# A hybrid decoder layer on one core: latent attention with its values made in token order, the keys of two heads in a bank of their own, its heads written out, and three weight splits moved

## The reference, cut to what matters

```python
x = x + 0.5 * swiglu(rms_norm(x, g1), ...)                  # up/gate 1024 -> 2816, down 2816 -> 1024
proj = rms_norm(x, g2) @ w_in                               # c_q 384, c_kv 256, k_rope 32, q_d/k_d/v_d, gates 2 x 1024
q  = rms_norm(c_q) @ w_uq      # 8 heads x (64 plain + 32 rotary)
kv = rms_norm(c_kv) @ w_ukv    # 8 heads x (64 for the key + 64 for the value)
y_a = causal_softmax(q, [k_nope, rope(k_rope)]) applied to v, then @ w_br_mla       # "latent attention"
y_b = dilated windowed attention of 3 x 8 heads @ w_br_dil
x = x + (sigmoid(g_a) * y_a + sigmoid(g_b) * y_b) @ w_out
x = x + 0.5 * swiglu(rms_norm(x, g3), ...)
y = rms_norm(x, g4)
```

## Time and profile before

| | us |
|---|---|
| median of 3 runs (1281.72 to 1281.84) | 1281.73 |
| the profiled execution's own time | 1280.79 |
| its span, first to last instruction | 1279.0 |
| PE busy in the span | 1267.3 (99%) |
| DVE, ACT, POOL busy | 669.7, 441.7, 18.8 |
| DMA | 118.38 MB, mean 93 GB/s |
| mean granted TensorE clock | 0.998 |

### The profile page before, as it was taken

The page is one execution under the profiler, slowest core; times in us unless marked ns, Lnnn a source line. Parts: engine busy times, 40 slices in busy tenths (PEclk is TensorE's granted clock), DMA queues, the critical chain, the costliest instruction groups (busy, mean ns, idle before and its releaser), DMA issues.

```text
span 1279.0 us, 16611 instructions
## 1 busy us (share of the span) xinstructions
PE 1267.3 (99%) x5998; PEld 1033.5 (81%) x5998; DVE 669.7 (52%) x984; ACT 441.7 (35%) x763; POOL 18.8 (1%) x36
## 2 busy tenths in 40 slices
PE   9999999999999999999999999999999999999997
PEld 6888888888888777788888888888888888888886
DVE  6744444433336677475665746675644444443323
ACT  6233332322233444343343424423433332232221
POOL 0000000000000000300000000000000000000000
PEclk9999999999999999999999999999999999999999
DMA  6342223333322221622222231222322322233321
GB/s 214 101 111 98 98 98 98 90 91 95 103 92 71 64 70 66 132 67 83 79 78 92 66 99 51 97 89 95 99 96 98 98 98 98 98 90 92 93 88 66
DMA packets 36003, 118.38 MB, mean 93 GB/s; under 512 B 4680, under 2 KB 4680, under 8 KB 35968
## 3 DMA queue, kind: packets, MB, share of 16 engines
q1 hardware_dynamic: 34416, 114.83, 27.8%
q0 software_dynamic: 1264, 3.06, 1.5%
q10 hardware_dynamic: 288, 0.03, 0.0%
HBM read 115.36 MB, written 2.55 MB: 92 GB/s over the span
## 4 chain that ended last, share of the span: by engine, by line
PE 94%; DVE 2%; DMA 1%; issue 1%; ACT 1%; SPq 0%; DVEq 0%; ACTq 0%
PE bank L542 36%; PE bank L376 17%; PE bank L378 17%; PE bank L377 17%; PE bank L725 1%; PE bank L751 1%; PE bank L645 1%; PE bank L672 1%; DVE mla_stats L1451 1%; DMA x<-in_x_t 1%; PE bank L661 1%; PE bank L769 1%; PE bank L765 1%; DMA const<-in_tables 0%; ACT w_hi L358 0%
## 5 line engine op out<-in xcount | busy, mean ns | idle before, releaser
L363 DVE TENSOR_TENSOR w_lo<-raw,w_hi 128x1024 fp32r<-128x1024 f32 (+2 forms) x221 | 258.8, 1171 | 227.6 <-ACT w_hi L358 225.4
L358 ACT ACTIVATE w_hi<-raw 128x1024 fp32r<-128x1024 f32 (+2 forms) x221 | 224.3, 1015 | 433.3 <-PE bank L542 228.3
L542 PE MATMUL bank<-act_hi,w_hi 128*128 128x512 f32 x704 | 218.5, 392 | 0.3 <-DVE w_lo L363 0.3
L542 PE MATMUL bank<-act_hi,w_lo 128*128 128x512 f32 x704 | 217.0, 389 | 0.0
L542 PE MATMUL bank<-act_lo,w_hi 128*128 128x512 f32 x704 | 216.9, 389 | 0.0
L376 PE MATMUL bank<-act_hi,w_hi 128*128 128x512 f32 x528 | 210.7, 399 | 2.0 <-DVE w_lo L363 1.2
L378 PE MATMUL bank<-act_hi,w_lo 128*128 128x512 f32 x528 | 206.2, 390 | 0.0
L377 PE MATMUL bank<-act_lo,w_hi 128*128 128x512 f32 x528 | 205.9, 390 | 0.0
L542 PEld LDWEIGHTS bank<-act_hi,w_hi 128*128 128x128 f32 x704 | 132.2, 188 | 29.6 <-DVE w_lo L363 1.0
L542 PEld LDWEIGHTS bank<-act_hi,w_lo 128*128 128x128 f32 x704 | 132.2, 188 | 27.5
L542 PEld LDWEIGHTS bank<-act_lo,w_hi 128*128 128x128 f32 x704 | 132.2, 188 | 27.4
(11 more groups left out here) (177 smaller groups left out, 1049.3 us busy)
## 6 DMA issues: line engine op xcount, KB each, us to landing
raw<-in_ffn_up SPq DMA_DIRECT2D x87, 512.0 KB, 3.3
raw<-in_w_dil SPq DMA_DIRECT2D x40, 512.0 KB, 3.3
raw<-in_ffn_down SPq DMA_DIRECT2D x32, 448.0 KB, 3.3
raw<-in_ffn_down SPq DMA_DIRECT2D x16, 512.0 KB, 3.5
raw<-in_w_mla_gates SPq DMA_DIRECT2D x8, 512.0 KB, 3.3
raw<-in_w_branches SPq DMA_DIRECT2D x8, 512.0 KB, 3.3
raw<-in_w_out SPq DMA_DIRECT2D x8, 512.0 KB, 3.2
raw<-in_w_latent SPq DMA_DIRECT2D x6, 512.0 KB, 3.3
```

The source lines that it names most:

```text
L358: nc.scalar.activation(w_hi[:, s % SPLIT, 0:tiles * P], raw[:, s % RAW, 0:tiles * P], ACT.Copy).then_inc(hi_ready, 1)
L363: nc.vector.tensor_tensor(w_lo[:, s % SPLIT, 0:tiles * P], raw[:, s % RAW, 0:tiles * P], w_hi[:, s % SPLIT, 0:tiles * P].bitcast(F32), ALU ...
L542: last = nc.tensor.matmul(out, w[:, s % SPLIT, tile * P:(tile + 1) * P], moving[:, row, :], start=row == 0 and w is w_hi and moving is act_hi,
```

## The change

- **Values.** A new piece `w_values` (8 tiles, the value columns of `w_ukv` for all heads) stands ahead of head 0. `values()` makes four chunks of 128 tokens by 512 value features, with the latents as the stationary and the weights as the moving operand: 4 x 2 x 3 = 24 matmuls of 128x512 into banks 5, 6, 2 and 3. ACT scales and copies them to `mla_v` in four activations. `turn_values`, `mla_vt`, L1444 and the copies of L1017 are gone.
- **Keys.** The keys of heads 2p and 2p+1 are one product of 2 tiles (6 matmuls) into bank 7, made with the query of head 2p; DVE takes both in `take_keys(p)`, which stands ahead of the scaling of head 2p-1. Pieces of even heads have 5 tiles, of odd heads 3. The gate chunk no longer shares a bank with keys.
- **Queries.** In even heads DVE takes the next query before the scaling of the probabilities, in odd ones after it.
- **Turning.** PE turns the first seven blocks before the eighth gate tile (k == 7) in even heads, before the seventh in odd ones.
- **Heads.** All eight are written out on every engine, without loops.
- **Splits.** In head 7 ACT rounds the second dilated piece before the exponentials, and DVE takes its remainder before the scaling. After each head ACT rounds the next gate piece before the tanh and no longer after it. In FFN 1, piece 4 is rounded before the first SiLU, and DVE takes its remainder right after its first product with that chunk.

The last hunk below is of DVE's `attention`, the others are PE's.

```diff
+            def values():
+                s = PIECES["mla"]
+                pe.wait_ge(lo_ready, s + 1)
+                pe.wait_ge(chunk_taken, CHUNKS["latent"] + 4)
+                for b, out in enumerate((5, 6, 2, 3)):
+                    block_of = slice(b * P, (b + 1) * P)
+                    for k in range(KKV):
+                        hi, lo = (w[:, s % SPLIT, k * SEQ:(k + 1) * SEQ] for w in (w_hi, w_lo))
+                        latent, rest = (part[:, KQ + k, block_of] for part in (lat_hi, lat_lo))
+                        nc.tensor.matmul(bank[out][:, :], latent, hi, start=k == 0, stop=False)
+                        nc.tensor.matmul(bank[out][:, :], latent, lo, start=False, stop=False)
+                        last = nc.tensor.matmul(bank[out][:, :], rest, hi, start=False, stop=k == KKV - 1)
...
+            def lora(h):
+                s = lora_piece(h)
+                pe.wait_ge(lo_ready, s + 1)
+                if h % 2 == 0:
+                    if h == 0:
+                        pe.wait_ge(mean_ready, 2)
+                    elif h > 2:
+                        pe.wait_ge(mixed_taken, h // 2 - 1)
+                    multiply(s, range(KQ, LORA_TILES), bank[7][:, :], lambda k: lat_hi[:, KQ + k, :],
+                             lambda k: lat_lo[:, KQ + k, :]).then_inc(inner_done, 1)
+                c = query_chunk(h)
+                free_chunk(pe, c)
+                multiply(s, range(KQ), bank[c % 2][:, :], lambda k: lat_hi[:, k, :],
+                         lambda k: lat_lo[:, k, :]).then_inc(piece_done, 1)
...
-            def turn_values(h, i):
...
             def score(h):
-                if h % 2:
-                    pe.wait_ge(turned_taken, 4 * h + 8 * i - 1)
                 pe.wait_ge(head_ready, h + 1)
+                if h == 0:
+                    pe.wait_ge(values_taken, BLOCKS)
...
             def attend(h):
+                if h < MLA_HEADS - 1:
+                    pe.wait_ge(keys_taken, h // 2 + 2)
...
                 def turn_early(k):
-                    if k == 6:
+                    if k == (6 if h % 2 else 7):
...
             def attention(h):
                 maxima(h)
+                if h == MLA_HEADS - 1:
+                    split_lo(dve, PIECES["dil"] + 1, 0, TILES)
+                    normalize(h)
+                    split_lo(dve, PIECES["dil"] + 2, 0, TILES)
...
+                    if h % 2:
+                        take_keys(h // 2 + 1)
+                        normalize(h)
+                        take_query(h + 1)
+                    else:
+                        take_query(h + 1)
+                        normalize(h)
```

More of the change, by code:

```diff
@@ L428, in _ @@
                 load(sp, PIECES["latent"] + q, 0, w_latent[q], TILES)
[L430 to L439, removed]
+            load(sp, PIECES["mla"], 0, w_values, TILES)
+            for h in range(MLA_HEADS):
+                at, tiles = (h % 2) * LORA_TILES * P, lora_tiles(h)
+                load(sp, lora_piece(h), 0, w_lora_up[h // 2, :, at:at + tiles * P], tiles)
+                load(sp, lora_piece(h) + 1, 0, w_mla_gates[h], TILES)
             with sp.Fori(0, PAIRS) as i:
@@ L609, in _ @@
             token_sums(sumsq, bank[7]).then_inc(norm_full, 1)
[L612 to L620, removed]
@@ L622, in turn_values @@
-            def turn_values(h, i):
[L625 to L631, removed]
-                if h % 2:
-                    pe.wait_ge(turned_taken, 4 * h + 8 * i - 1)
-                pe.wait_ge(head_ready, h + 2 * i + 1)
+            def values():
[10 more added lines that the diff above has]
+                        last = nc.tensor.matmul(bank[out][:, :], rest, hi, start=False, stop=k == KKV - 1)
+                    if b < BLOCKS - 1:
+                        last.then_inc(values_done, 1)
+                last.then_inc(piece_done, 1)
@@ L1053, in _ @@
[L1053 to L1057, removed]
+                    split_hi(act, PIECES["dil"] + 1, 0, TILES)
+                exponentials(h)
+                if h < MLA_HEADS - 2:
+                    split_hi(act, lora_piece(h + 2), 0, lora_tiles(h))
+                elif h == MLA_HEADS - 2:
+                    split_hi(act, PIECES["dil"], 0, TILES)
+                else:
+                    split_hi(act, PIECES["dil"] + 2, 0, TILES)
@@ L1255, in up_turn @@
                             dve.wait_ge(own, so_far())
-                    else:
+                    elif not (first and f == 0):
                         split_lo(dve, s + 2, 4 * i, TILES)
@@ L1780 @@
     up_q = given["w_uq"][0].reshape(Q_LORA, MLA_HEADS, QK_DIM)
-    up_kv = _tiles(given["w_ukv"][0])
+    up_kv = given["w_ukv"][0].reshape(KV_LORA, MLA_HEADS, QK_NOPE + V_DIM)
+    put("w_values", up_kv[:, :, QK_NOPE:].reshape(KKV, P, MLA_HEADS * V_DIM).transpose(1, 0, 2).reshape(P, TILES * P))
     rows = []
-    for h in range(MLA_HEADS):
-        query = np.concatenate([up_q[:, h, :QK_NOPE], _swapped(up_q[:, h, QK_NOPE:])], axis=1)
-        rows.append(np.concatenate([_tiles(query)[0], up_kv[h]], axis=1))
+    for pair in range(MLA_HEADS // 2):
+        first, second = (_tiles(np.concatenate([up_q[:, h, :QK_NOPE], _swapped(up_q[:, h, QK_NOPE:])], axis=1))[0]
+                         for h in (2 * pair, 2 * pair + 1))
+        keys = _tiles(up_kv[:, 2 * pair:2 * pair + 2, :QK_NOPE].reshape(KV_LORA, 2 * QK_NOPE))[0]
+        rows.append(np.concatenate([first, keys, second], axis=1))
     put("w_lora_up", np.stack(rows))
```

234 lines of the change are left out of this document (116 added, 118 removed).

## The result

The changed kernel takes 1273.01 us in the median of 4 runs (1272.48 to 1273.69), the kernel before 1281.78 beside it (4 runs, 1281.72 to 1283.47): a ratio of 0.9929, 95% interval 0.9911 to 0.9946. Timed again in a later comparison it took 1272.84 against 1281.23, ratio 0.9933 (0.9916 to 0.9949). The profiled executions took 1280.79 and 1272.62, 8.2 us apart.

The account below looks back on a forecast made before the run. PE, busy 99% of the span, was taken as the bound. Terms 3.0 + 1.4 + 1.3 + 0.3 - 0.2 = 5.8 us took the median from 1281.73 to 1275.9 us; range 1274.3 to 1278.6.

Parts of the forecast that it names:

- transposes: Eight heads each lose four PE transposes of the values, 0.38 us a head: 3.0 us saved, bounds 2.1 and 3.7.
- the gate's bank: PE's gate matmul no longer waits for DVE to empty a shared bank in heads 0, 1, 3, 5: 1.4 us saved.
- head 7: PE's wait between the two dilated pieces goes because the second is split earlier: 1.3 us saved, at least 1.2.
- first turn: PE's idle time before piece 4 goes with its split ahead of the SiLU: 0.3 us saved, bounds 0 and 0.4.
- even heads: DVE's scaling ends only 0.15 us ahead of PE's need: 0.05 us lost a head, 0.2 in all, at most 1.2.
- What bounds the kernel: Whole span: PE is busy 99%, so only what PE issues or waits for is on the path.
- Matmuls: Key, value and query products: 120 matmuls of 128x512 before and after, only moved, nothing gained or lost.
- The start of the stage: Ahead of head 0, the added value matmuls bring no PE wait: cost 0, cover 0.9 us.
- the DVE-late rival: Scaling ends late in heads 0, 2, 4, 6, 0.5 to 0.7 us each: gain only 3.2 us, 1278.5; chance 0.10.
- bank 7 as a wait: `attend` waits some 1.4 us for `keys_taken` four times, total 1281.5; chance 0.05, with other such waits.
- unhidden fetches: Instructions of four more written-out head bodies arrive late, 12 us in all: slower, 1287.9; chance 0.03.
- it leaves little: Removing the heads' loops may gain, but only 0.78 us of idle exists in all heads, 0.4 of it head 0's.

Follow-up runs that it names:

- own_bank_late: Kernel before with heads written out, and key and value products in bank 7 except in head 0: 1279.45 against 1281.23 us, ratio 0.9988.
- head7_splits: Kernel before with only head 7's rounding moved ahead of the exponentials and its remainder ahead of the scaling: 1279.90 against 1281.36 us, ratio 0.9988.
- transposes_twice: Kernel before with eight transposes of the values per head in place of four: 1281.61 against 1281.36 us, ratio 0.9999.

## Why the prediction was right in kind and too small

| term | forecast | measured | by |
|---|---|---|---|
| transposes | 3.0 | 4.1 | put back into the changed kernel |
| the gate's bank | 1.4 | 2.0 with the loops written out, and 0.2 ahead of head 0 | own_bank_late; the two traces |
| head 7 | 1.3 | 1.5 | head7_splits |
| first turn | 0.3 | 0.35 | distances of starts |
| even heads | -0.2 | 0 | no wait in the trace after |
| sum | 5.8 | 8.15 | profiled executions: 8.2 |

That the sum meets the 8.2 so closely is in part luck: the terms come from different runs. Between the two traces the latent attention alone is 8.0 us shorter, where its terms give 7.8, and the first turn's 0.35 (375.72 to 375.37 us from the table products to the latents) shows as 0.1 in the window ahead, because the changed kernel's profiled execution came to the table products 0.23 us later (31.55 for 31.32), which varies from run to run (32.23 when the same kernel ran again).

- **What bounds the kernel**: right. The gain is PE's own time and what PE waited for, and outside the latent attention only the first turn moved by more than 0.1 us.
- **Matmuls**: right, 120 and 120.
- **Transposes: mis-sized, the largest miss.** The prediction argued "I take 3.0, since starts are what PE pays", and counted from the first transpose's start to the next matmul's start. It left out what a group does to its neighbours: 0.10 us a head lies in the scores ahead of it, because the weight load of the group's first transpose starts later than a 128-row load does there, and about 0.03 lies behind. It is 0.52 a head and not 0.38, above even the bound of 3.7. The bound went by shown lengths of the group alone and had no room for its neighbours. The 275 ns for each that the Trainium skill gives ("TensorE: Matmul & The Clock Gate", Part 4: PE-mode transpose) would have made an estimate of 8.8. The runs give 4.1 for 32, so starts were the better guide, and one neighbour was missing.
- **The gate's bank: mis-sized.** "Less 0.23 that is 0.56 and 0.29" counts the gap alone. Behind a gap PE is slow for a while longer: 18 matmuls in 4.23 us for 4.08, 0.15 in each of four heads. The row shows it, 0.49 us for the first gate matmul at 423.39 and 437.01; the same group of rows gave me the 0.12 for the bound of the transposes, and I didn't apply it here. The distances from the start of one group to the start of the next contain both, the gap alone does not. The 2.0 is a price for the bank and the loops together; the bank with the loops kept wasn't run.
- **Head 7, first turn**: right in kind; the 0.2 over the forecast in head 7 is mostly the same slow start.
- **The start of the stage**: right, no wait came, and the value matmuls hide one (`mean_ready`), which the prediction didn't name as cover.
- **Even heads**: right in the place and in how narrow it is; the 0.2 us charged for it did not come. PE finds the scaling done, by a hair, and three matmuls sooner it doesn't.
- **Loads and the rivals**: the DVE-late rival, bank 7 as a wait and unhidden fetches all fail. The text said of the loops that "it leaves little". They did cost 0.78 us in the trace, too little for the medians to tell, through the chain of ACT and DVE that the gate waited for and through a later start of PE behind DVE. With a bank of its own PE doesn't wait there, so this is part of the 2.0 and no further gain; that is argued from the waits that are gone.
- **Adding terms**: the sum was right to add them, but by luck of the change. In the kernel before, transposes in heads 0, 1, 3, 5 and 7 stood ahead of a wait for DVE that swallows PE's work (transposes_twice: 0.72 us for 32 more, where 8 x 0.25 would be 2.0). That taking the transposes away alone would have returned little in these heads is argued from this and wasn't run.

The lower end of the range, 1274.3, stands 0.6 us below what the upper bounds add up to (1274.9), and the prediction gives no term for it; the result is below both.

The median moved by 8.8 in the first comparison, 8.4 in the second, the profiled executions by 8.2; the kernel before alone scatters by 1.8 us in the first comparison, so the three don't contradict each other.

## What to carry to other kernels

Price a group of small matmuls by the start of the group before it to the start of the group behind it, and compare with a place where the group is absent or the wait doesn't happen (here heads 2, 4, 6 against 1, 3, 5); its own length misses what it does to its neighbours. Before adding up what edits save on the bound engine, ask of each whether a wait for another engine stands right behind it: there the saving counts only if that wait goes too. When a margin comes out at 0.15 us, the run one step tighter shows whether the arithmetic was right.

## What the runs showed of the hardware that I had not expected

- A group of four transposes of 64 rows behind a 128-row matmul cost more than one of 128 rows: 0.52 us a head against 0.39 (stage 111.35 and 110.33 against 107.22, eight heads). Its first weight load starts 0.58 and not 0.43 us after the one before. At a change between 128 and 64 columns 0.10 us was lost too (scores 2.66 for 2.56 us, load and matmul both at 447.64).
- After a stop PE's first load and matmul started together (a load at 423.39 beside the matmul at 423.39 in the kernel before), and the 18 matmuls behind it took 0.13 to 0.15 us longer than without a stop.
- An ACT operation addressed by a loop's register started 0.52 us after the operation before, with a constant address 0.39 or 0.40. PE started 0.14 us after the end of the DVE operation it waited for in the loop, and 0.06 in the same place written out.
